# Weight chunks of a float32 decoder trunk loaded in pairs: one 1 MB transfer into two neighbouring ring slots

## The reference, cut to what matters

```python
mod = einsum('bd,sdk->bsk', silu(c), ada_w[i]) + ada_b[i]        # 2 x 2048 x 6144 weights a layer
h = modulate(rmsnorm(x, norm_g[i, 0]), shift_t, scale_t)
y = pool_mixer(h, pool_w, pool_scale) or retention(h, ret_w_in, ret_w_out)   # 2048 x 12288, 4096 x 2048
x = x + gate_t * y
h = modulate(rmsnorm(x, norm_g[i, 1]), shift_m, scale_m)
a = relu(h @ mlp_w1[i]); x = x + gate_m * ((a * a) @ mlp_w2[i])  # 2048 x 8192, 8192 x 2048
```

## Time and profile before

| what | value |
|---|---|
| median of 3 runs | 2342.3 us (2341.7 to 2342.43) |
| the profiled execution | 2342.16 us, its span 2340.3 us |
| PE, PEld busy | 2251.3 us (96%), 1816.1 us (78%) |
| DVE, ACT busy | 1680.3 us (72%), 1083.6 us (46%) |
| queue of SP | 611.92 MB, 75.6% of the 16 DMA engines' span |
| mean granted PE clock | 0.987 |

### The profile page before, as it was taken

One profiled execution on the slowest core, in us unless ns is written; L12 is line 12 of the kernel. 1 busy time (PEld: TensorE's weight loads), 2 busy tenths in 40 slices (PEclk: granted clock), 3 DMA queues, 4 the chain that ended last, 5 costly groups with the idle time before them and its releaser, 6 DMA issues.

```text
span 2340.3 us, 28469 instructions
## 1 busy us (share of the span) xinstructions
PE 2251.3 (96%) x10017; PEld 1816.1 (78%) x10017; DVE 1680.3 (72%) x1809; ACT 1083.6 (46%) x1340; POOL 138.9 (6%) x248
## 2 busy tenths in 40 slices
PE   4489999999999999999999999999999999999998
PEld 2147788888888887888888888887888888888887
DVE  4668888788887898767676767677877555555556
ACT  2324554544544545444454444445543453453454
POOL 0000000100100100001000001000100000000000
PEclk9689999999999999999999999999999999999999
DMA  9999989998998977878767877866897776776774
GB/s 401 415 413 396 337 294 327 369 362 283 367 330 298 362 275 251 305 246 269 244 224 234 298 242 247 271 231 204 328 361 244 241 229 195 226 231 191 232 227 150
DMA packets 276530, 664.21 MB, mean 284 GB/s; under 512 B 21752, under 2 KB 22184, under 8 KB 269360
## 3 DMA queue, kind: packets, MB, share of 16 engines
q1 hardware_dynamic: 260320, 611.92, 75.6%
q0 software_dynamic: 15184, 49.87, 6.2%
q10 hardware_dynamic: 896, 0.75, 0.1%
HBM read 638.30 MB, written 24.14 MB: 283 GB/s over the span
## 4 chain that ended last, share of the span: by engine, by line
PE 86%; DVE 3%; DMA 3%; issue 1%; ACT 1%; POOL 0%; POOLq 0%; SPq 0%; DVEq 0%; ACTq 0%
PE acc L699 84%; DMA raw<-in_mlp_w 3%; DVE w_lo L1574 1%; PE acc L1100 1%; ACT w_hi L1151 0%; PE score_ps L1087 0%; DVE ada_acc L1580 0%; DMA scratch<-in_decay 0%; DVE h_lo L1830 0%; PE score_ps L887 0%; PE tb L827 0%; DVE ev L1876 0%; PE tb L961 0%; DVE h_hi L1828 0%; DVE x L1880 0%
## 5 line engine op out<-in xcount | busy, mean ns | idle before, releaser
L1574 DVE TENSOR_TENSOR w_lo<-raw,w_hi 128x1024 fp32r<-128x1024 f32 x775 | 943.6, 1223 | 559.2 <-ACT w_hi L1151 556.6
L1151 ACT ACTIVATE w_hi<-raw 128x1024 fp32r<-128x1024 f32 x775 | 821.8, 1061 | 1100.3 <-PE acc L699 972.8
L699 PE MATMUL acc<-w_hi,h_lo 128*128 128x512 f32 x1788 | 698.4, 391 | 3.3 <-issue 1.6
L699 PE MATMUL acc<-w_hi,h_hi 128*128 128x512 f32 x1788 | 696.0, 389 | 0.0
L699 PE MATMUL acc<-w_lo,h_hi 128*128 128x512 f32 x1788 | 695.7, 389 | 0.0
L699 PE MATMUL acc<-w_hi,a_lo 128*128 128x512 f32 x1312 | 513.2, 391 | 2.5 <-DVE a_lo L2273 2.1
L699 PE MATMUL acc<-w_lo,a_hi 128*128 128x512 f32 x1312 | 511.8, 390 | 0.0
L699 PE MATMUL acc<-w_hi,a_hi 128*128 128x512 f32 x1312 | 511.5, 390 | 0.0
L699 PEld LDWEIGHTS acc<-w_hi,h_lo 128*128 128x128 f32 x1788 | 335.7, 188 | 75.7 <-issue 4.9
L699 PEld LDWEIGHTS acc<-w_hi,h_hi 128*128 128x128 f32 x1788 | 335.6, 188 | 70.2
L699 PEld LDWEIGHTS acc<-w_lo,h_hi 128*128 128x128 f32 x1788 | 335.7, 188 | 68.6
(11 more groups left out here) (198 smaller groups left out, 896.1 us busy)
## 6 DMA issues: line engine op xcount, KB each, us to landing
raw<-in_mlp_w SPq DMA_DIRECT2D x512, 512.0 KB, 5.1
ada_raw<-in_ada_w SPq DMA_DIRECT2D x248, 512.0 KB, 6.8
raw<-in_ret_w_in SPq DMA_DIRECT2D x192, 512.0 KB, 4.7
ada_early_h<-in_ada_w SPq DMA_DIRECT2D x32, 1024.0 KB, 13.5
raw<-in_ret_w_out SPq DMA_DIRECT2D x64, 512.0 KB, 4.5
ada_raw<-in_ada_w SPq DMA_DIRECT2D x16, 1024.0 KB, 12.5
square_blocks<-ev POOLq DMA_DIRECT2D x112, 128.0 KB, 4.8
ev<-square_blocks POOLq DMA_DIRECT2D x28, 512.0 KB, 6.2
```

The costliest lines, as they stand in the source:

```text
L699: mm = nc.tensor.matmul(acc[pair][t][:], l[:, CK * c + j, tok], w[:, slot, j, :], start=first and j == 0 and i == 0, stop=last and j == CK ...
L1151: nc.scalar.activation(w_hi[:, o % RING], raw[:, o % RING], ACT.Copy).then_inc(hi_ready, 1)
L1574: nc.vector.tensor_tensor(w_lo[:, o % RING], raw[:, o % RING], w_hi[:, o % RING].bitcast(F32), ALU.subtract).then_inc(lo_ready, 1)
```

## The change

After the prelude, and except for the 3 chunks that follow chunk 0 of the first half unit, SP loads two chunks with one transfer of 1 MB into slots 0 and 1 or 2 and 3. `load_two(o)` waits for `lo` of chunk o-3 (the last reader of the second slot) where `load_chunk(o)` waited for `lo` of chunk o-4. It counts up the semaphore of the even slot only; `hi` of both chunks waits on that one. `ada` loads that stood between the two chunks now stand behind both. The source functions take a number of chunks. Of the 776 chunks, 12 are still loaded alone (8 of `pool_w`, 4 of the first half unit); 764 come in 382 transfers. Nothing changes on PE and DVE.

```diff
+            def load_two(o, source):
+
+                sp.wait_ge(lo_ready, n.of("U") * HALF + (o + 1 - RING + 1))
+                sp.dma_start(raw[:, o % RING:o % RING + 2].rearrange("p s k n -> p (s k) n"),
+                             source).then_inc(raw_in[o % RING], 16)
...
                 for o in range(CH - c0):
-                    load_chunk(o, source(c0 + o))
+                    if o % 2 == 0:
+                        load_two(o, source(c0 + o, 2))
                     for a in behind.get(o, []):
                         load_ada(seg, a)
...
-                return lambda c: weights[c * CK * P:(c + 1) * CK * P, col].rearrange("(k p) n -> p k n", p=P)
+                return lambda c, chunks=1: weights[c * CK * P:(c + chunks) * CK * P, col].rearrange("(k p) n -> p k n", p=P)
...
-                    load_chunk(s, source(s))
+                    if i == 0:
+                        load_chunk(s, source(s))
+                    elif s % 2 == 0:
+                        load_two(s, source(s, 2))
                 n.unit("p1")
...
                                 for s, (v, c) in enumerate(PAIR_W2):
-                                    load_chunk(s, sources[v](c))
+                                    if s % 2 == 0:
+                                        load_two(s, sources[v](c, 2))
...
-            def hi(o):
+            def hi(o, alone=False):
 
                 u = n.of("U")
-                act.wait_ge(raw_in[o % RING], (u + (o // RING + 1)) * 16)
+                act.wait_ge(raw_in[o % RING if alone else o % RING // 2 * 2], (u + (o // RING + 1)) * 16)
```

More of the change, by code:

```diff
@@ L580, in rows_of @@
             def rows_of(weights, col):
-                return lambda c: weights[c * CK * P:(c + 1) * CK * P, col].rearrange("(k p) n -> p k n", p=P)
+                return lambda c, chunks=1: weights[c * CK * P:(c + chunks) * CK * P, col].rearrange("(k p) n -> p k n", p=P)
             def group_rows_of(weights, g, block_):
                 grouped = weights.rearrange("(g k p) n -> g p k n", k=KT, p=P)
-                return lambda c: grouped[bass.ds(g, 1), :, c * CK:(c + 1) * CK,
-                                         block_ * NB:(block_ + 1) * NB].rearrange("g p k n -> p (g k) n")
+                return lambda c, chunks=1: grouped[bass.ds(g, 1), :, c * CK:(c + chunks) * CK,
+                                                   block_ * NB:(block_ + 1) * NB].rearrange("g p k n -> p (g k) n")
             for a in range(RING):
@@ L1328, in _ @@
             modulated(0)
-            hi(0)
-            hi(1)
+            hi(0, True)
+            hi(1, True)
             modulated(1)
@@ L1334, in _ @@
             pooled_hi(1)
-            hi(2)
-            hi(3)
+            hi(2, True)
+            hi(3, True)
             modulated(3)
@@ L1339, in _ @@
             pooled_hi(3)
-            hi(4)
-            hi(5)
+            hi(4, True)
+            hi(5, True)
             evacuate_group(0)
-            hi(6)
-            hi(7)
+            hi(6, True)
+            hi(7, True)
             evacuate_group(1)
```

## The result

| kernel | median, us | runs | ratio to before |
|---|---|---|---|
| before | 2342.02 (2341.69 to 2342.43) | 5 | |
| changed | 2428.07 (2423.26 to 2434.65) | 5 | 1.0364 [1.0353, 1.0375] |

The change costs 86 us, 3.6%. The forecast was 2343.8 us, no change, and its range ended at 2353. The changed kernel's profiled execution took 2429.4 us, with a span of 2427.6.

What follows compares the result with a forecast made beforehand. The prediction took PE to bound the kernel, with 86% of the chain of waits. Half units +1.0, rotations +0.2 and +0.4 made +1.6 us on the profiled 2342.2: 2343.8 us, range 2340.8 to 2353.

Steps and rivals of the forecast that it cites:

- The light stages: Stages with little other traffic: the later, paired loads were to cost nothing, covered by 5.8 us.
- Room: Light stages: time between a chunk's `w_lo` being ready and PE needing it, put at 5.8 us.
- The landing of 1 MB: Light stage: a pair's time from issue to data in, taken as 5.7 us, between 5.6 and 8.6.
- Stages with `ada` pieces: 340 to 850 and 1645 to 1790 us: room used in bursts, then refilled; cost 0, bounds 0 and 11 us.
- the limits: Longest landing the four-chunk ring bears within PE's 10.9 us: 7.3 us, or 6.0 with an `ada` sum between.
- Waits for `w_lo` alone: Whole kernel: the sign of being right was PE's wait for `w_lo` growing from 2.7 to 4 or 5 us.
- Half units: 190 to 275 us, DMA saturated: even chunks land 1.31 us later, stalling PE; +1.0 us, bounds 0 to 4.
- L: Time from a load's issue to its landing; the ring's round was L + 2.3 before, L + 3.6 or 4.9 with pairs.
- Rotations: Retention: nothing at seven rotations, +0.2 us at one, and +0.4 us at the first, which waits for a table.
- Rival B: Slower: the ring cycle becomes the bound once L averages over about 6.7 us, PE stalls; 2355 us, chance 0.20.
- Rival C: Faster: larger transfers raise the saturated rate, giving PE back 1.45 us in the half units; 2340.8 us, chance 0.12.
- Rival D: Fully hidden: the half units' stalls vanish in PE's existing 1.45 us wait; 2342.3 us, chance 0.18.

Runs made afterwards that it cites:

- E8: Kernel before, with pairs only in chunks 584 to 775, the light part of the last MLP, where no `ada` pieces are loaded: 2342.31 us, 1.0000.
- E9: Changed kernel, each pair as two 512 KB transfers issued at the pair's time, `hi` of the even chunk waiting for both: 2422.02 us, 1.0340.
- E3: Kernel before, single loads at their old times, `ada` loads that stood behind an even chunk moved behind the odd one: 2348.84 us, 1.0023.
- E11: Changed kernel, in retention (all units but the first) ACT's other work of a step put ahead of `hi` instead of behind: 2429.88 us, 1.0373.
- E1: Changed kernel, each pair as two 512 KB transfers issued at the pair's time, `hi` of each chunk waiting only for its own data: 2366.01 us, 1.0094.
- E10: Kernel before, old issue times, `ada` loads behind the odd chunk, `hi` of an even chunk waiting for both chunks' data: 2367.32 us, 1.0103.

## Why the prediction was wrong, step by step

**The light stages: right.** Room 5.8 us, landing 5.7 us, cost nothing. Measured: landing 5.4 us, cost 0 in 192 chunks (E8, and the last line of the stage table).

**The landing of 1 MB, 5.7 us: right where it was derived, and of no use elsewhere.** The Trainium skill ("DMA: Bandwidth & Descriptors", section "Bandwidth") lists 6.15 us for 1 MB, measured on transfers that GpSimd issued, and its rule is to batch to at least 1 MiB. The 5.4 us measured here, for transfers that SP issued, is lower than that figure, and E9 against the changed kernel shows nothing gained by the batch.

**Stages with `ada` pieces, cost taken 0, bounds 0 and 11: the step that failed, +50 us.** The landing was put at 5.7 to 7.5 us, and the limits at 7.3 and 6.0 us. But the landing of raw loads of the changed kernel in 420 to 720 is this:

```profile
DMA to landing us min/median/max: 5.0/7.1/10.3
```

The median is over 6.65, the mean of the two limits that the prediction used for its upper bound, and yet it wrote that the room "will be used" and "refilled". In a ring, room is refilled only by rounds shorter than PE's 10.9 us. Of the 51 rounds begun in this window 36 are over 10.95 and the median is 12.0 us; in the kernel before it was 37 of 111, with a median of 10.9. So the deficits add up until the room is gone; from there each one is paid. The bound of 11 us took 0.35 us a round; one round of the 450 to 500 stretch lies six times that over PE's 10.9. The changed kernel's timeline:

```profile
463.88 0.38 SPq L522 DMA_DIRECT2D raw<-in_mlp_w  x1
...
476.99 0.38 SPq L522 DMA_DIRECT2D raw<-in_mlp_w  x1
...
472.32 2.00 ACT L1162 ACTIVATE w_hi<-raw 128x1024 fp32r<-128x1024 f32 x2 [6.05 <-DMA raw<-in_mlp_w]
...
473.41 1.23 DVE L1585 TENSOR_TENSOR w_lo<-raw,w_hi 128x1024 fp32r<-128x1024 f32 x1 [4.50 <-ACT w_hi L1162]
474.55 1.28 DVE L1591 SCALAR_TENSOR_TENSOR ada_acc<-ada_raw,cond,ada_acc 128x1024 f32<-128x1024 f32 x1
475.75 1.22 DVE L1585 TENSOR_TENSOR w_lo<-raw,w_hi 128x1024 fp32r<-128x1024 f32 x1
```

Landing 8.4 us, tail 4.7, round 13.1 us: 2.2 over PE's. DVE stood idle for 4.5 us in the middle of it, though it is the engine that the prediction named as the busy one ("DVE is at 42 of 50 us"). It waits, then has three instructions in a row that the next load waits for.

**Waits for `w_lo` alone: too narrow.** The room was counted for one consumer. But `hi` waits in ACT's queue, and a wait there holds up everything behind it, and so does a late `lo` on DVE. The changed kernel at 530, ACT, DVE, then PE:

```profile
530.88 2.01 ACT L1162 ACTIVATE w_hi<-raw 128x1024 fp32r<-128x1024 f32 x2 [4.52 <-DMA raw<-in_mlp_w]
532.79 1.13 ACT L1405 ACTIVATE a_hi<-ev 128x512 fp32r<-128x512 f32 x2
...
534.25 1.28 DVE L1591 SCALAR_TENSOR_TENSOR ada_acc<-ada_raw,cond,ada_acc 128x1024 f32<-128x1024 f32 x1
535.44 1.29 DVE L2151 TENSOR_TENSOR a_lo<-ev,a_hi 128x512 fp32r<-128x512 f32 x2
...
536.88 0.77 PE L710 MATMUL acc<-w_hi,a_lo 128*128 128x512 f32 x1 [4.35 <-DVE a_lo L2151]
```

ACT sat 4.5 us in front of `hi`, and `a_hi` of the next rows of the w2 stage, which needs no weights at all, stood behind it. Its partner `a_lo` stood on DVE behind two `lo` and a sum. PE waited 4.35 us for it. In the MLP of layer 0 PE waits 16.1 us for `a_lo`, in 6 places, and 11.6 for `w_lo`, in 15. The prediction asked of a wait on SP what stands behind it, and found `ada` loads; of ACT's new waits it did not ask.

**Half units, "+1.0", bounds 0 to 4: measured +9.** The reckoning had L = 6.7 us, and with it a round of 11.6 us, already 0.7 over PE's 10.9. It was not carried on over the stage's seven or eight rounds, but settled by where two chunks would be tight. Measured: landing 7.1 us in the median, rounds of 12.1 (9.1 to 13.6). The rounds of the kernel before had a median of 11.75 us here and were paid out of PE's lead, as the prediction said, so a round that is too long is not by itself new; what is new is that it got longer and the lead did not last. "The total of bytes stays, and the queue stays full" was wrong too: 379 GB/s for 399. With a pair issued only when both slots are free, four slots hold at most two loads; that the queue then drains between them is my reading of the lower rate. E9, with the same issue times and two transfers, moves 377 GB/s there, and E3, with the old ones, 398. Some 2 of the 9 us are the `ada` order (E3).

**Rotations, "+0.2" and "+0.4": measured +29 in retention, of which only 5 at the rotations.** The first pair behind a rotation was put at `hi` 1.3 us early. The changed kernel's timeline of such a place, ACT, DVE, PE's weight loads:

```profile
1133.55 2.01 ACT L1162 ACTIVATE w_hi<-raw 128x1024 fp32r<-128x1024 f32 x2 [6.88 <-DMA raw<-in_ret_w_in]
1137.40 2.01 ACT L1162 ACTIVATE w_hi<-raw 128x1024 fp32r<-128x1024 f32 x2 [1.84 <-DMA raw<-in_ret_w_in]
1139.31 1.07 ACT L1178 ACTIVATE ev<-acc 128x512 f32<-128x512 f32 x2
...
1141.97 0.68 DVE L2223 TENSOR_TENSOR scratch<-ev,scratch 128x512 f32<-128x512 f32 x1
...
1147.45 3.45 DVE L1585 TENSOR_TENSOR w_lo<-raw,w_hi 128x1024 fp32r<-128x1024 f32 x3
...
1148.68 0.19 PEld L710 LDWEIGHTS acc<-w_hi,h_lo 128*128 128x128 f32 x1 [1.83 <-DVE w_lo L1585]
```

The pair was issued at 1126.13 and in at 1133.55, 7.4 us, where the prediction had 6.3 (1070.86 + 1.13 to 1078.3). PE had ended its unit at 1136.4, but ACT stood before `hi` of the next pair until 1137.40, so the evacuation began at 1139.31, the rotation at 1141.97, the next `lo` at 1147.45, and PE's weight load waited 1.8 us. The prediction did name that risk ("or the next rotation starts late against its 0.7 us") and then took seven of eight rotations at nothing. PE waits for `w_lo` behind five of the eight, 6.3 us in all for 1.2 before.

More, 13.7 us, is lost at four groups of score matmuls (2.8 to 3.9 us each), for which the prediction had no term and where the kernel before does not wait. One of them, ACT and then PE:

```profile
1172.21 1.06 ACT L1162 ACTIVATE w_hi<-raw 128x1024 fp32r<-128x1024 f32 x1 [3.98 <-DMA raw<-in_ret_w_in]
1173.18 1.13 ACT L1526 ACTIVATE scratch<-scratch 128x512 f32<-128x512 f32 x2
...
1174.41 2.90 PE L1098 MATMUL score_ps<-scratch 128*128 128x256 f32 x8 [3.52 <-issue]
```

ACT stood 4 us before `hi`, behind it in its queue stood the scaling of the scores' operand, and PE started when that was done; E11 is the test of it. The remaining 10 us of the 29 are slower matmuls behind the waits and small gaps; they were not taken apart.

**Rival B** had the mechanism and its starting point, L = 6.7 us, and gave it a chance of 0.20. It is what happened. Its price, 5 + 2 + 4 us on top of the 1.6, came from a bound that took a round to lose 0.35 us and from half a us at each rotation, and took only `w_lo` to be late; measured were 41, 9 and 29. So even with B as the forecast the time, 2355, would have been 73 us short. **Rival C** fails: the saturated rate fell. **Rival D** fails: +9 in the half units.

**What the rows at hand would have said.** The round of before was L + 2.3, 8.6 us at the median landing of 6.3 us, and 12.7 at the longest of 10.4, so it already went over PE's 10.9 at times (37 of 111 rounds in 420 to 720 us were over 10.95). The tail grows from 2.3 to 3.6 or 4.9, and the landing by the second half megabyte. What decides in the stages with `ada` pieces, as far as these runs show, is how many rounds in a row then lie over 10.9 us, not whether the median lies near it. In retention the count alone does not tell the kernels apart (77 of 126 rounds, 138 of 262 before), where rotations and scores break the rounds up; there what stands behind the waits has to be looked up. The later issue and the whole landing cost 17 and 18 us even alone (E1 and E10 against E3).

## What to carry to other kernels

In a ring of four, joining two slots in one transfer takes away half of the loads that can be in flight: the first slot's load goes out later and its data counts later, and the two together cost twice the sum of each alone (73 us for 17 and 18), so that each alone looks cheap and both together are not. Compare the time from issue to reissue of a slot, with all that stands between on every queue, with the consumer's time for the ring, stage by stage, and where it is longer multiply by the number of rounds. And ask of every engine that gets a new wait, not only of the one that issues the loads, what stands behind it in its queue.

## What the runs showed that was not expected

**PE's granted clock falls behind most of the long waits.** The changed kernel has 7 waits of PE of over 2.5 us (the kernel before has none behind 190 us). Busy time by short stretches (columns of the earlier trace rows), around two of them:

```profile
532.00:536.00 4.00, 0.53 (x3) 0.10 (x1) 4.00 (x4) 3.06 (x5) 0.00 (x0) 0.93 1.04 411
536.00:540.00 4.00, 3.12 (x7) 2.48 (x8) 4.00 (x5) 0.87 (x1) 0.00 (x0) 0.50 1.00 379
540.00:544.00 4.00, 4.00 (x14) 3.20 (x13) 1.87 (x3) 1.06 (x1) 0.00 (x0) 0.72 0.73 215
...
1172.00:1176.00 4.00, 1.59 (x4) 1.35 (x5) 1.94 (x2) 3.04 (x4) 0.00 (x0) 0.71 1.03 395
1176.00:1180.00 4.00, 4.00 (x13) 3.33 (x12) 3.16 (x6) 0.00 (x0) 0.00 (x0) 0.50 0.67 216
```

PE had stood still for 4.35 us (532.5 to 536.9) and for 3.5 us (1170.9 to 1174.4). In 536 to 540 and in 1176 to 1180 the granted clock is 0.50, the 1.2 GHz level, and matmuls are listed with 0.63 us instead of 0.39. Six of the seven long waits are followed by 2 to 12 trunk matmuls at about double spacing (0.43 us), 43 in all; that is 9 us of the 15 us of wide spacing above. The eight score matmuls at 1174.41 take 2.90 us, where such a group takes 1.47 in the kernel before. So a wait costs PE its own length and some 1.5 us more. The length of a wait alone does not decide it: behind the seventh, 2.8 us at 1028.7, the clock stays, and in E9 it stays behind waits of 2.65 and 3.6 us but falls behind others of 1.85 and 2.1. That the fall is caused by the standstill is read from their order in time; no run here takes the clock away by itself.

**512 KB transfers lose nothing against 1 MB.** At the same times and waits, two of 512 KB and one of 1 MB differ by 6 us in 2428 (E9), in favour of the small ones if at all. A lone pair's 5.4 us against a lone chunk's 4.3 shows what the second half costs there: 1.1 us.
